# Queries 1 and 2 as one pair of products ahead of the attention, the later queries two steps sooner, six gate products beside the attention

## The reference

```python
h = rms_norm(x, norm_mix_g)
proj = h @ w_in          # q_a (8 heads of 64), six k/v of 128, g_nsa, q_b (8 heads of 64), k_b, v_b, g_merge (2 x 1024)
kc, vc = compress_blocks(k_cmp), compress_blocks(v_cmp)
o_cmp = compressed_branch(q_a, kc, vc);  o_slc = selected_branch(q_a, k_slc, v_slc);  o_win = banded_attention(q_a, k_win, v_win, 256)
o_a = g[..., 0] * o_cmp + g[..., 1] * o_slc + g[..., 2] * o_win
o_b = banded_attention(q_b, k_b, v_b, 128, sinks)
gate_a, gate_b = split(sigmoid(g_merge))
x = x + (gate_a * (o_a @ w_a) + gate_b * (o_b @ w_b)) @ w_o
```

## Time and profile before

| what | us |
| --- | --- |
| median of 3 runs | 2913.58 (2907.95 to 2914.45) |
| the profiled execution's own time | 2906.41 |
| its span | 2904.5 |
| TensorE busy | 2811.6 |
| VectorE busy | 1742.2 |
| ScalarE busy | 583.0 |
| GpSimd busy | 297.3 |

### The profile page before, as it was taken

One profiled execution on the slowest core, in us unless ns is written; L12 is line 12 of the kernel. 1 busy time (PEld: TensorE's weight loads), 2 busy tenths in 40 slices (PEclk: granted clock), 3 DMA queues, 4 the chain that ended last, 5 costly groups with the idle time before them and its releaser, 6 DMA issues.

```text
span 2904.5 us, 34196 instructions
## 1 busy us (share of the span) xinstructions
PE 2811.6 (97%) x13472; PEld 2173.2 (75%) x13472; DVE 1742.2 (60%) x3727; ACT 583.0 (20%) x1278; POOL 297.3 (10%) x284
## 2 busy tenths in 40 slices
PE   8999999999999999999999899999999999999985
PEld 7888887578888877888865587888877766885321
DVE  6557767875656366676348766676356445664213
ACT  1101011122221031221022412221022464001001
POOL 0000020020000100000101430000100373001110
PEclk9999999999999999999999999999999999999998
DMA  5232333112213221232221111232223201257997
GB/s 214 85 112 88 128 130 109 58 59 94 109 65 119 100 88 68 77 116 102 87 76 58 44 59 66 87 116 100 89 73 107 90 16 59 87 238 288 424 425 326
DMA packets 61732, 351.33 MB, mean 121 GB/s; under 512 B 8576, under 2 KB 14848, under 8 KB 22784
## 3 DMA queue, kind: packets, MB, share of 16 engines
q1 hardware_dynamic: 45184, 322.98, 29.1%
q10 hardware_dynamic: 11776, 17.71, 1.7%
q0 software_dynamic: 4608, 8.40, 0.8%
HBM read 339.62 MB, written 14.16 MB: 122 GB/s over the span
## 4 chain that ended last, share of the span: by engine, by line
PE 90%; DVE 4%; DMA 2%; SPq 2%; ACT 1%; issue 1%; POOL 0%; DVEq 0%; ACTq 0%; POOLq 0%
PE bank L931 43%; PE bank L1159 23%; PE bank L541 6%; PE bank L550 4%; PE bank L3981 2%; DMA ring<-in_weights 2%; SPq L3921 2%; PE bank L2828 2%; PE bank L579 2%; PE bank L2812 1%; PE bank L3415 1%; PE bank L4000 1%; PE bank L571 1%; PE bank L3050 0%; PE bank L674 0%
## 5 line engine op out<-in xcount | busy, mean ns | idle before, releaser
L931 PE MATMUL bank<-area,mixed 128*128 128x256 f32 x2264 | 507.9, 379 | 1.9 <-DVE mixed L953 1.9
L931 PEld LDWEIGHTS bank<-area,mixed 128*128 128x128 f32 x2264 | 429.8, 190 | 60.8 <-DVE mixed L953 2.4
L931 PE MATMUL bank<-area,ring 128*128 128x256 f32 x1536 | 346.3, 379 | 0.1
L931 PEld LDWEIGHTS bank<-area,ring 128*128 128x128 f32 x1536 | 291.6, 190 | 40.5 <-DVE area L972 0.5
L953 DVE TENSOR_TENSOR mixed<-ring 128x512 f32<-128x512 f32 (+2 forms) x117 | 80.8, 690 | 306.8 <-PE bank L931 299.9
L1159 PE MATMUL bank<-area 128*128 128x256 f32 x1080 | 242.9, 379 | 0.0
L1159 PEld LDWEIGHTS bank<-area 128*128 128x128 f32 x1080 | 205.2, 190 | 27.9
L1159 PE MATMUL bank<-buf_a,area 128*128 128x256 f32 x800 | 183.3, 379 | 0.0
L1159 PE MATMUL bank<-buf_b,area 128*128 128x256 f32 x760 | 175.5, 379 | 0.0
L1159 PEld LDWEIGHTS bank<-buf_a,area 128*128 128x128 f32 x800 | 152.0, 190 | 20.7
L931 PE MATMUL bank<-buf_b,mixed 128*128 128x256 f32 x744 | 167.3, 379 | 0.0
(11 more groups left out here) (633 smaller groups left out, 4166.1 us busy)
## 6 DMA issues: line engine op xcount, KB each, us to landing
ring<-in_weights SPq DMA_DIRECT2D x236, 1024.0 KB, 4.8
area<-in_weights SPq DMA_DIRECT2D x35, 1024.0 KB, 28.2
buf_b<-in_weights SPq DMA_DIRECT2D x10, 1024.0 KB, 27.2
buf_a<-in_weights SPq DMA_DIRECT2D x8, 1024.0 KB, 25.9
const<-in_weights SPq DMA_DIRECT2D x5, 1024.0 KB, 27.5
norm<-in_weights SPq DMA_DIRECT2D x4, 1024.0 KB, 23.7
mixed<-in_weights SPq DMA_DIRECT2D x4, 1024.0 KB, 27.5
area<-area ACTq DMA_DIRECT2D x20, 128.0 KB, 2.4
```

The source lines that it names most:

```text
L931: mm = pe.e.matmul(b, w[:, k * P:(k + 1) * P], x(INPUT_OF[p], unit.lo + k), start=(unit.key, BANK_OF[p]) not in begun, stop=unit.last and ...
```

## The change

`EARLY_QUERIES` goes from 2 to 3. Queries 1 and 2 become a fourth pair of seven half-width parts ahead of `kc`, in place of query 1's single product there and of query 2's four parts inside the attention. ScalarE scales queries 0, 1 and 2 in place after their pairs. The four-part queries that are left, 3 to 7, lie at steps 4 to 23. The gate unit's parts lie at steps 26, 28, 31, 32, 33 and 34, with part 6 at step 34. The weights' packing follows: one whole block for the new pair in place of the eight pieces of query 1 and of query 2.

```diff
-EARLY_QUERIES = 2
+EARLY_QUERIES = 3
...
-          "b_pair_cin", "b_pair_key", "b_pair_last")
+          "b_pair_cin", "b_pair_key", "b_pair_last", "b_pair_query")
...
-    outs = [(((BKC, P),), ((BVC, P),)), (((BKS, P),), ((BKW, P),)), (((BKB, P),), head_columns(BQA, 0))]
+    outs = [(((BKC, P),), ((BVC, P),)), (((BKS, P),), ((BKW, P),)), (((BKB, P),), head_columns(BQA, 0)),
+            (head_columns(BQA, 1), head_columns(BQA, 2))]
...
-    plan["b_pair_last"], plan["b_compress_1"] = pairs[2:], compress[1]
-    plan["b_query_next"] = queries[1:EARLY_QUERIES]
+    plan["b_pair_last"], plan["b_compress_1"], plan["b_pair_query"] = pairs[2:3], compress[1], pairs[3:]
...
-    GATE_PARTS, GATE_BANKS, GATE_MIXED_AT = {29: 1, 30: 2, 31: 4, 32: 5, 33: 7}, (QUERY_BANK, 0, 1), 24
+    GATE_PARTS, GATE_BANKS, GATE_MIXED_AT = {26: 1, 28: 2, 31: 4, 32: 5, 33: 7, 34: 6}, (QUERY_BANK, 0, 1), 24
...
-        j, part = divmod(s + 6, 4)
+        j, part = divmod(s + 8, 4)
...
         compress(1)
-        for j in range(1, EARLY_QUERIES):
-            product(pe, stream, g, ("q", j), plan["b_query_next"][j - 1], x)
+        pair(3)
...
         ac.wait_ge(*read_of(B_PAIRS[2])[1])
-        ac.e.activation(n_q[:, 0, :], n_q[:, 0, :], ACT.Copy, scale=C("q_scale", 0, 1)).then_inc(q_done, 1)
+        scaled_query(0)
         compressed(1)
+        pair_first(3)
+        ac.wait_ge(*read_of(B_PAIRS[3])[3])
         for j in range(1, EARLY_QUERIES):
-            query(j)
+            scaled_query(j)
...
         pair(2, n_keys[:, 2, :], n_q[:, 0, :])
+        pair(3, n_q[:, 1, :], n_q[:, 2, :])
```

More of the change, by code:

```diff
@@ L856, in counts_before @@
         return [sum(COUNTS[name][what] for name in earlier) for what in range(3)]
-    PAIRED = ("cin", "key", "last")
+    PAIRED = ("cin", "key", "last", "query")
     def merged_at(way, n):
@@ L3320, in plan_nsa @@
             g.add(("hid", 1, m), (hid_done, 2 + m + 1), blocks=B("b_compress_1", m))
-        for j in range(1, EARLY_QUERIES):
-            g.add(("q", j), (q_done, j + 1), blocks=B("b_query_next", j - 1))
+        pair(3)
         g.add(("kc",), (kc_done, KD + 2), blocks=B("b_compress_k", 0))
@@ L3476, in scalar_nsa, with scaled_query @@
         pair_first(2)
+        def scaled_query(j):
+            ac.e.activation(n_q[:, j, :], n_q[:, j, :], ACT.Copy, scale=C("q_scale", j, j + 1)).then_inc(q_done, 1)
         ac.wait_ge(*read_of(B_PAIRS[2])[1])
-        ac.e.activation(n_q[:, 0, :], n_q[:, 0, :], ACT.Copy, scale=C("q_scale", 0, 1)).then_inc(q_done, 1)
+        scaled_query(0)
         compressed(1)
+        pair_first(3)
+        ac.wait_ge(*read_of(B_PAIRS[3])[3])
         for j in range(1, EARLY_QUERIES):
-            query(j)
+            scaled_query(j)
         att_n.scalar(ac, lambda e, item, o: e.e.activation(n_q[:, item["tile"], :], o, ACT.Copy), late_query)
```

## The result

| kernel | median, us | runs | ratio to before |
| --- | --- | --- | --- |
| before, beside the change's first runs | 2910.62 (2907.95 to 2914.45) | 8 | |
| changed | 2919.09 (2916.51 to 2921.04) | 8 | 1.0028 (95%: 1.0017 to 1.0039) |
| changed, again, in a later group (before: 2911.38) | 2919.02 | 9 | 1.0027 (1.0017 to 1.0037) |

The change makes the kernel slower by 0.28%, some 8 us; the forecast was +4.05 us. The median of 2919.09 us lies in the forecast's range (2911.5 to 2923.0), and the predicted time of 2917.6 us came near it partly by luck: it was carried over from a median of three runs (2913.58) that lies 3 us above the median of eight.

What follows compares the result with a forecast made beforehand. TensorE, busy 97% of the span, was taken as the bound except where it stands idle. The terms +5.2 - 1.65 + 0.5 = +4.05 us gave 2917.6 us, range 2911.5 to 2923.0.

Steps and rivals of the forecast that it cites:

- (b): Thin TensorE stretches at steps 2 to 3 and 24 to 26 fall to half clock, up to +1.7 us each; chance 0.22.
- Part 1: Ahead of the attention: a pair replaces query 1's single product, +5.2 us on the path, with VectorE's and ScalarE's extra work hidden.
- Part 2: Start of the attention: two query parts of 1.72 us leave steps 2 and 3, gaining 1.65 us.
- Part 3, up to step 26: Steps 24 and 25: 3.45 us of query products leave, but VectorE's mix holds the time; only 0.1 us comes off.
- Part 3, steps 26 to 31: Gate products moved to steps 26 and 28 delay the value products; +0.5 us in sum with steps 24 and 25.
- Gate part 6 at step 34: Sixth gate product, issued behind the last value products where it already stands: no move, zero cost.
- (a): TensorE bounds everything, so only the saved products count: 1.7 us less, 2911.9 us; chance 0.15.
- (c): Gate products find no cover because ScalarE's queue runs late, and the start gains at most 0.5: +6.4 us, 2920.0; chance 0.13.
- the fourth block of 12.1 us: Sign in the profile: a fourth block of half-width products before the attention, taking 12.1 us.
- the missing wait of step 27: Sign in the profile: TensorE's 1.12 us wait before step 27's value products is gone, filled by step 26's gate product.
- the new stretches at half clock: Sign in the profile: one or two more stretches at clock 0.5 would show the half-clock rival, (b).

Runs made afterwards that it cites:

- e6: Changed kernel with only VectorE's mix (the sums of the gate's weights) moved from step 24 to 22: 2914.16 us, ratio 1.0017.
- e4: Changed kernel plus products nobody reads, one at each of steps 2 and 3, two at each of 24 and 25: 2916.28 us, ratio 1.0019.
- e1: Changed kernel with queries 3 to 7 back at steps 6 to 25 and gate products back at 29 to 33: 2914.31 us, ratio 1.0015.
- e2: Changed kernel with VectorE's mix of the gate's weights moved from step 24 to 14: 2918.46 us, ratio 1.0025.
- e9: Changed kernel with queries 3 to 7 at steps 2 to 21, mix at step 20, gate products at 29 to 33: 2911.62 us, ratio 1.0003.
- e5: Kernel before the change with queries 2 to 7 at steps 0 to 23 and the mix at step 22: 2909.66 us, ratio 0.9998.

## Why the prediction was right and wrong

The direction was right, and so was the walk for the pair and for the tail. The size was half: +4.05 us forecast, +8 measured. The ratio of 1.0028 lies outside "within 0.2%", to which the forecast gave 0.72, though its interval (from 1.0017) does not shut 0.2% out. What happened is rival (b), at 0.22, and on top of it the term for the start of the attention was too good.

- **Part 1, +5.2 us: right.** 5.21 to 5.23 in every profile with the pair. The helpers on VectorE and ScalarE are hidden (0.83 us left over of the forecast 0.9). Behind the attention the two profiles run alike to 0.2 us, so the weight traffic cost nothing, as said.
- **Part 2, -1.65 us: wrong.** This is the term that failed. At full clock, from the scores of step 2 to those of step 4, emptying the steps gave 0.24 us. The transposes' second bank was overlooked: the step said "TensorE then goes straight through both transposes", but they wait 1.23 us for ScalarE's copy out of the bank they need, and that copy stands behind the exponentials. Then the fall at step 4 took 1.37 us, which is rival (b) and not part of this term. That step 5 shows only +0.14 us in all is owed to the 0.99 us that before's own fall lends. In the other profile the same points give +2.35 us, with a fall of 10.2 us from step 0.
- **Part 3, up to step 26, -0.1 us: right.** Measured -0.02: 3.45 us of products taken out, nothing gained, the mix as the cause (e6: with the mix covered, 2.4 us are gained).
- **Part 3, steps 26 to 31, +0.6 us (+0.5 with the -0.1): right as a walk, mis-sized by the clock.** 2.05 us in the changed kernel, 0.70 with idle products in place of the gap (e4).
- **Gate part 6 at step 34: right, no move.** Steps 31 to 34 are equally late in the changed kernel.
- **(a)** is refuted by e1: the same products on TensorE, 3.8 to 4.8 us less. **(c)** gave the right kind of time for the wrong reason; the evacuation of query 7 delayed nothing that TensorE waited for.
- **(b)** named steps 2 and 3 and steps 24 to 26, and "up to +1.7 us" for each fall. The falls came at steps 4 and 26 and cost 1.37 and 1.35 us.
- **The sum.** By the profile the terms are 5.23 - 0.99 - 0.24 + 1.37 - 0.02 + 2.05 = 7.4 us. The second profile gives 9.6, the medians 7.6 to 8.5. The changed profile's span is 10.9 us longer. 3.2 us of this lie ahead of the first pair, and so ahead of everything that was changed: 1.7 of them are a fall at about 2201.4 us, in a product of 10.15 us (8.46 before). It shows the run and not the change: e6's and e1's profiles have it too, e2's, e4's and e9's have not.

Of the signs named in advance, the fourth block of 12.1 us, the missing wait of step 27 and the new stretches at half clock came. TensorE was idle 2.7 of 6.90 us between steps 24 and 26, behind the maxima and the copy that the mix had held up. The attention was to be 1.0 to 1.3 us shorter than 160.7 us; it was 2.2 longer.

The Trainium skill's rule in the forecast ("TensorE: Matmul & The Clock Gate", Part 1: The HAM clock gate), that the clock goes by how busy TensorE has been lately and has two levels, agrees with the rows at 0.54 and 0.53. The forecast held it right to give this a rival, and wrong to give it 0.22: its own walk had TensorE idle 3 us of 6 in steps 24 to 26, more than in the stretch ahead of the fall in the earlier trace rows (3.57 busy of 4.50).

## What to carry to other kernels

Work that lies beside a chain of waits is not free to move out of it: each piece covers something, and before it is taken away the longest instruction on the other engines' queues in that step has to be moved or covered too (here one line, the mix from step 24 to 22, was worth 3.8 us in the profiles, and the pair 1.6 over two single products). Products that are moved from beside a wait to where TensorE is the bound cost their full time there and give back only what the other engines leave. Where a change thins out TensorE's work, put the half clock into the sum as a term for each thin stretch, and not only as a rival: 3.4 us at half clock cost 1.0 to 1.6 us here. And before a step of one profile is compared with the same step of another, see whether both had the same falls ahead of it.

## What the runs showed that I had not expected

- Products of 0.86 us that nobody reads cost nothing in the gap at steps 24 and 25, and the clock stayed full there: 1.35 us saved in the profile. With the two at steps 2 and 3, after which no fall came either, the kernel was 2.8 us faster by the medians.
- The same program falls to half clock in different places from run to run. Of 13 profiles, nine have a fall within the first step or two of the attention, and it lasts 3.4, 6.8 or 10.2 us. The kernel before alone has runs of two kinds in the group with e5, 4 us apart.
- The falls behind emptied steps are not of that kind: eight of eight profiles with steps 2 and 3 empty have one at step 3 or 4, and none of the other five.
- Between two falls a step's distance to the same step of another kernel repeats to 0.02 us over 17 steps and on more than one chip, so single profiles tell tenths of a microsecond where medians of eleven runs tell three.
